# Hybrid decoder layer on one core: bias table read backwards by its user, per-tile roots of q and k, and several steps moved by a few slots

## Time and profile before

| what | value |
|---|---|
| median of 3 runs | 790.46 us (788.77 to 791.02) |
| profiled execution, own time | 790.41 us |
| its span | 788.7 us |
| mean granted TensorE clock | 0.969 |
| instructions in the span | 9486 |
| VectorE, ScalarE, GpSimd busy | 478.9, 338.8, 91.7 us |
| read of the bias table: issued, time to landing | 33.8 us, 8.0 us |
| first layer-norm transposes | 320.6 us |
| end of the plan (first feed-forward product) | 423.4 us |

### The profile page before, as it was taken

How to read it: one execution, slowest core, us unless ns; L and a number is a source line. 1 busy time by engine, 2 the same in 40 slices (tenths; PEclk the granted TensorE clock), 3 DMA queues, 4 the chain that set the end, 5 groups by cost and what they waited for, 6 DMA issues and landing times.

```text
span 788.7 us, 9486 instructions
## 1 busy us (share of the span) xinstructions
PE 738.3 (94%) x3442; PEld 588.2 (75%) x3446; DVE 478.9 (61%) x725; ACT 338.8 (43%) x508; POOL 91.7 (12%) x75
## 2 busy tenths in 40 slices
PE   3999978599989989799997999999999999999998
PEld 2766757477766778587875888888888888888886
DVE  5246797996799866666655565655656656222222
ACT  6244637187855576263334334344343443211110
POOL 2000364753100001303010000000000000000000
PEclk9999998799999999999996999999999999999999
DMA  8431132222211141102231133233332332333202
GB/s 260 151 139 55 54 106 54 54 62 91 63 53 54 55 160 54 53 16 92 81 108 53 54 106 84 78 105 106 106 96 74 96 106 106 107 106 107 82 26 106
DMA packets 78047, 69.46 MB, mean 88 GB/s; under 512 B 5815, under 2 KB 64535, under 8 KB 78015
## 3 DMA queue, kind: packets, MB, share of 16 engines
q1 hardware_dynamic: 77871, 68.51, 28.2%
q10 hardware_dynamic: 144, 0.52, 0.2%
HBM read 66.91 MB, written 2.12 MB: 88 GB/s over the span
## 4 chain that ended last, share of the span: by engine, by line
PE 72%; DVE 10%; issue 8%; ACT 4%; POOL 4%; DMA 1%; SPq 0%; DVEq 0%; POOLq 0%; ACTq 0%
PE bank L1454 62%; PE bank L1460 3%; POOL stats L730 3%; DVE u_acc L569 2%; PE bank L1474 2%; DVE w_lo L579 1%; DMA x_in<-in_x 1%; PE bank L1649 1%; PE bank L1625 1%; PE bank L1592 1%; DVE xbcT L1261 1%; DVE q_tok L1224 1%; POOL u_acc L751 1%; DVE k_tok L1224 1%; DVE h_lo L1090 1%
## 5 line engine op out<-in xcount | busy, mean ns | idle before, releaser
L1454 PE MATMUL bank<-h_hi,w_hi 128*128 128x512 f32 x480 | 191.3, 398 | 1.8 <-DVE h_lo L1090 1.8
L1454 PE MATMUL bank<-h_lo,w_hi 128*128 128x512 f32 x480 | 188.0, 392 | 0.0
L1454 PE MATMUL bank<-h_hi,w_lo 128*128 128x512 f32 x480 | 188.0, 392 | 0.0
L579 DVE TENSOR_TENSOR w_lo<-w_raw,w_hi 128x2048 fp32r<-128x2048 f32 x34 | 78.6, 2312 | 80.7 <-ACT w_hi L820 80.7
L1454 PEld LDWEIGHTS bank<-h_hi,w_hi 128*128 128x128 f32 x480 | 90.7, 189 | 28.4 <-issue 9.9
L1454 PEld LDWEIGHTS bank<-h_hi,w_lo 128*128 128x128 f32 x480 | 90.7, 189 | 19.6
L1454 PEld LDWEIGHTS bank<-h_lo,w_hi 128*128 128x128 f32 x480 | 90.9, 189 | 18.1
L1415 DVE SCALAR_TENSOR_TENSOR f<-bank,prm,f 128x511 f32<-128x511 f32 x88 | 65.8, 748 | 58.3 <-ACT f L1059 52.0
L820 ACT ACTIVATE w_hi<-w_raw 128x2048 fp32r<-128x2048 f32 x34 | 64.9, 1910 | 78.3 <-PE bank L1454 78.0
L1059 ACT ACTIVATE f<-bank,prm 128x512 f32<-128x512 f32 x44 | 33.8, 769 | 102.4 <-PE bank L1454 102.4
L1454 PE MATMUL bank<-w_hi,g_hi 128*128 128x512 f32 x176 | 68.5, 389 | 0.0
(11 more groups left out here) (231 smaller groups left out, 1049.8 us busy)
## 6 DMA issues: line engine op xcount, KB each, us to landing
w_raw<-in_w_up SPq DMA_DIRECT2D x44, 512.0 KB, 4.7
w_raw<-in_w_in SPq DMA_DIRECT2D x34, 512.0 KB, 4.6
w_raw<-in_w_down SPq DMA_DIRECT2D x22, 512.0 KB, 4.0
w_raw<-in_w_out SPq DMA_DIRECT2D x12, 512.0 KB, 4.3
x_in<-in_x SPq DMA_DIRECT2D x4, 512.0 KB, 6.8
trev<-distance_table SPq DMA_DIRECT2D x1, 2048.0 KB, 8.0
x<-in_x SPq DMA_DIRECT2D x4, 512.0 KB, 6.8
out_x<-y_out SPq DMA_DIRECT2D x8, 256.0 KB, 2.0
```

The source lines that it names most:

```text
L579: eng.tensor_tensor(wlo[:, slot, cols], wraw[:, slot, cols], whi[:, slot, cols].bitcast(F32), ALU.subtract).then_inc(ready, 1)
L1454: ins = pe.matmul(o, a, b, start=first and i == 0 and q == 0, stop=last and i == n - 1 and q == 2)
```

## The change

The one-hot table is made for distances the other way round, so that the read from memory lands directly in `tbias`, and `logit` reads a head's row backwards, from column W-1 to 0. `trev`, `jrev`, the `tbias` steps on TensorE and ScalarE and their two constants' instructions on GpSimd go. The read into `tbias`, which lies where x was, also waits for the four normalised tiles.

`qkms` and `qkn` are done per token tile: the tile's 8 sums are scaled in the slot that summed them, its root is 128 x 8, and its normalising stands ahead of the slot after the next.

Convolution taps of tiles 1, 2 and 3 end in slots 50, 63 and 65 instead of 52, 66 and 69. Layer norm moves from slots 70 and 71 to 66 and 67 (`lnn` follows one slot later), its transposes back from 73 and 74 to 70 and 71. The scan's four chunks start in slots 68, 72, 76 and 80 instead of 66, 70, 74 and 78. `silux` and `cs` move from slot 62 to 64, `xt` from 63 to 65, `siluz` from 68 to 70.

```diff
@@ -61,7 +61,7 @@
 
 def bucket_onehot():
 
-    n = np.maximum(511 - np.arange(NG), 0)
+    n = np.maximum(np.arange(NG) - (P - 1), 0)
     nf = np.maximum(n, 1).astype(np.float32)
     half = NBUCKET // 2
     large = half + (np.log(nf / np.float32(half)) / np.float32(np.log(MAXDIST / half))
@@ -72,9 +72,10 @@
 
 
 TOP_SLOTS = {1: (9, 36), 2: (9, 42), 3: (9, 48)}
-DW_SLOTS = [(15, 44), (14, 52), (42, 66), (46, 69)]
-LN_SLOT = 69
-SSD_SLOTS = (66, 70, 74, 78)
+DW_SLOTS = [(15, 44), (14, 50), (42, 63), (46, 65)]
+LN_SLOTS = (66, 66, 67, 67)
+LNT_SLOTS = (70, 70, 71, 71)
+SSD_SLOTS = (68, 72, 76, 80)
 DW_POOL = 0
 
 
@@ -143,15 +144,13 @@
         fill[TOP_SLOTS[b][1]].append(("sel", b))
 
     put(1, ("gtab",))
-    for h in range(NH):
-        put(11 + h, ("tbias", h))
 
     for w, what in enumerate("qk"):
         n = at[(what, 1)]
         for t in range(NT):
             put(n + 1 + t, ("qkev", what, t))
-        fill[n + 4].append(("qkms", what))
-        front[n + 7].append(("qkn", what))
+            fill[n + 1 + t].append(("qkms", what, t))
+            front[n + 3 + t].append(("qkn", what, t))
         put(n + 8, ("qkT", what, 0), ("qkT", what, 1))
         put(n + 9, ("qkT", what, 2), ("qkT", what, 3))
     for t in range(NT):
@@ -181,23 +180,22 @@
         spread([("dw", j, i) for i in range(CONV_K)], a, b)
         if j == DW_POOL:
             spread([("dwp", j, i) for i in range(1, CONV_K)], a - 1, b - 1)
-    d2 = LN_SLOT
     for t in range(NT):
-        put(d2 + 1 + t // 2, ("ln", t))
-        front[d2 + 2 + t // 2].append(("lnn", t))
+        put(LN_SLOTS[t], ("ln", t))
+        front[LN_SLOTS[t] + 1].append(("lnn", t))
     for j in range(4):
-        put(d2 + 4 + j // 2, ("lnT", j))
+        put(LNT_SLOTS[j], ("lnT", j))
 
     for m in range(8):
         n = at[("xbc", 0)] + 2 * m + 2
         put(n, ("xbase", m))
         put(n + 1, *[("xtap", m, i) for i in range(1, SK)])
-    s0 = at[("z", 0)] + 2
+    s0 = at[("z", 0)] + 4
     put(s0, ("silux",), ("cs",))
     put(s0 + 1, *[("xt", t) for t in range(NT)])
     for t in range(NT):
         put(at[("z", 1)] + 1 + t, ("ev", "z", t))
-    put(at[("z", 1)] + 4, ("siluz",))
+    put(at[("z", 1)] + 6, ("siluz",))
     for t, n in enumerate(SSD_SLOTS):
         put(n, ("csr", t))
         front[n + 1].append(("seg", t))
@@ -251,7 +249,7 @@
 
     for s in PLAN:
         k = s[0]
-        if k in ("prm", "tbias", "idx", "ln", "lnT", "qkT", "cs", "iwT", "yT"):
+        if k in ("prm", "idx", "ln", "lnT", "qkT", "cs", "iwT", "yT"):
             aux.append(s)
         elif k == "score":
             aux += [("score", s[1], e) for e in range(2)]
@@ -392,8 +390,6 @@
         oneh = at("onehot_sb", [NBUCKET, NG], F32, r5)
         relb = at("relb", [NBUCKET, NH], F32, r5 + 2560)
         gsb = at("gsb", [NH, NG], F32, r5 + 3 * K)
-        jrev = at("jrev", [P, P], F32, r5 + 6 * K)
-        trev = at("trev", [P, NH, 512], F32, r6)
         tbias = at("tbias", [P, NH, 512], F32, r2)
 
         iqT = at("iqT", [P, 2, SEQ], F32, r3)
@@ -667,7 +663,8 @@
 
                     finished(sp, "hT", NT - 1, 1)
                     src = bass.AP(gdram.tensor, 0, [[1, P], [NG, NH], [1, 512]])
-                    sp.dma_start(trev[:, :, :], src).then_inc(s_trev, 16)
+                    sp.wait_ge(xn_ready, NT)
+                    sp.dma_start(tbias[:, :, :], src).then_inc(s_trev, 16)
                 elif s == ("xt", 0):
 
                     for e in range(2):
@@ -716,14 +713,11 @@
             link(pool.affine_select(out=tri[:, :], in_=ones[:, :], compare_op=ALU.is_ge, fill=0.0,
                                     base=0, pattern=[[1, P]], channel_multiplier=-1))
             link(pool.memset(neg_l[:, :], 0.0))
-            link(pool.memset(jrev[:, :], 0.0))
             link(pool.affine_select(out=neg_q[:, :], in_=neg_l[:, :], compare_op=ALU.is_ge,
                                     fill=MASKED, base=0, pattern=[[-1, P]], channel_multiplier=1))
             link(pool.affine_select(out=neg_l[:, :], in_=neg_l[:, :], compare_op=ALU.is_ge,
                                     fill=MASKED, base=0, pattern=[[1, P]], channel_multiplier=-1))
-            pool.affine_select(out=jrev[:, :], in_=jrev[:, :], compare_op=ALU.not_equal, fill=1.0,
-                               base=-(P - 1), pattern=[[1, P]], channel_multiplier=1)\
-                .then_inc(s_const, 1)
+            pool.sem_inc(s_const, 1)
 
             def inverse_root(out_, in_, ready):
                 n = out_.free_size()
@@ -736,10 +730,9 @@
                     pool.wait_ge(ms_ready, t + 1)
                     inverse_root(rstd[:, t:t + 1], ssq[:, t:t + 1], rstd_ready)
                 elif k == "qkms":
-                    which = "qk".index(s[1])
-                    pool.wait_ge(qkms_ready, which + 1)
-                    inverse_root(rqk[:, 32 * which:32 * which + 32],
-                                 ssqk[:, 32 * which:32 * which + 32], rqk_ready)
+                    i = NT * "qk".index(s[1]) + s[2]
+                    pool.wait_ge(qkms_ready, i + 1)
+                    inverse_root(rqk[:, NH * i:NH * i + NH], ssqk[:, NH * i:NH * i + NH], rqk_ready)
                 elif k == "dw" and s[1] == DW_POOL:
 
                     _, j, i = s
@@ -882,9 +875,6 @@
                     act.activation(dtl, dtu, ACT.Ln).then_inc(dtl_ready, 1)
                 elif k == "hi":
                     split_hi(s[1])
-                elif k == "tbias":
-                    finished(act, *s)
-                    drain(act.activation(tbias[:, s[1], :], ps(*s)[:, :], ACT.Copy), *s)
                 elif k == "idx":
                     _, b, h = s
                     i = (b - 1) * NIH + h
@@ -1207,30 +1197,28 @@
                                       sqs[:, i % 2, :].rearrange("p (h c) -> p h c", h=NH),
                                       AX_X, ALU.add).then_inc(sq_used, 1)
                 elif k == "qkms":
-                    w = "qk".index(s[1])
-                    dve.wait_ge(sq_used, NT * (w + 1))
+                    i = NT * "qk".index(s[1]) + s[2]
+                    dve.wait_ge(sq_used, i + 1)
 
 
                     a, b = (1.0, HD * EPS) if s[1] == "q" else (1.0 / HD, EPS)
-                    c = ssqk[:, 32 * w:32 * w + 32]
+                    c = ssqk[:, NH * i:NH * i + NH]
                     dve.tensor_scalar(c, c, a, b, ALU.mult, ALU.add).then_inc(qkms_ready, 1)
                 elif k == "qkn":
-                    w = "qk".index(s[1])
-                    tok = q_tok if s[1] == "q" else k_tok
-                    dve.wait_ge(rqk_ready, w + 1)
-                    for t in range(NT):
-                        v3 = tok[:, t, :].rearrange("p (h c) -> p h c", h=NH)
-                        c = 32 * w + NH * t
-                        dve.tensor_tensor(v3, v3, rqk[:, c:c + NH].unsqueeze(2)
-                                          .to_broadcast([P, NH, HD]), ALU.mult).then_inc(qkn_ready, 1)
+                    _, what, t = s
+                    i = NT * "qk".index(what) + t
+                    tok = q_tok if what == "q" else k_tok
+                    dve.wait_ge(rqk_ready, i + 1)
+                    v3 = tok[:, t, :].rearrange("p (h c) -> p h c", h=NH)
+                    dve.tensor_tensor(v3, v3, rqk[:, NH * i:NH * i + NH].unsqueeze(2)
+                                      .to_broadcast([P, NH, HD]), ALU.mult).then_inc(qkn_ready, 1)
                 elif k == "logit":
                     _, u, b, hp = s
                     W = P * (b + 1)
                     if u == 0:
 
                         finished(dve, "qkT", "k", 3)
-                        for hh in range(NH):
-                            evacuated(dve, "tbias", hh)
+                        dve.wait_ge(s_trev, 16)
                     if u > 1:
 
                         finished(dve, "turn", u - 2, turn_banks((u - 2) // NPAIR) - 1)
@@ -1239,7 +1227,7 @@
                         finished(dve, "score", u, e)
                         drain(dve.tensor_tensor_reduce(
                             prob[:, u % 2, e, 0:W], ps("score", u, e)[:, 0:W],
-                            tbias[:, 2 * hp + e, 384 - P * b:384 - P * b + W], -1.0, 3.4e38, ALU.add, ALU.min, mn[:, i:i + 1]), "score", u, e)
+                            tbias[:, 2 * hp + e, W - 1::-1], -1.0, 3.4e38, ALU.add, ALU.min, mn[:, i:i + 1]), "score", u, e)
                 elif k == "share":
                     u = s[1]
                     dve.wait_ge(exp_ready, 2 * u + 2)
@@ -1586,11 +1574,6 @@
                                   first=whole or i == 0, last=whole or i == 1)
                     if whole or i == 1 or q == 3:
                         ins.then_inc(acc_step, 1)
-                elif k == "tbias":
-                    pe.wait_ge(s_trev, 16)
-                    claim(pe, *s)
-                    pe.matmul(ps(*s)[:, :], jrev[:, :], trev[:, s[1], :], start=True, stop=True)\
-                        .then_inc(aux_done, 1)
                 elif k == "idx":
```

## The result

The changed kernel takes 768.56 us (median of 4 executions, 767.84 to 770.06) against 789.62 for the kernel before (4 executions, 788.63 to 791.02): ratio 0.9734, 95% interval 0.9711 to 0.9758, that is 21 us less. The forecast was 763.6, range 755 to 775. The profiled execution is the slowest of the four, 770.06 us with a span of 768.3, so that the two traces differ by 20.4.

A forecast was written before the change was run, and what follows sets the result against it. TensorE's busy time and idle waits bound the kernel, with VectorE's queue setting the first stretch's pace once those waits go. 22.3 - 1.5 + 0 + 6.5 - 0.5 = 26.8 us off 790.4 gives 763.6, range 755 to 775.

The forecast's parts named there:

- Bias table: TensorE's eight pairs of products with the anti-identity go, 0.86 us each: 6.9 us.
- Reversed read: 32 logits on VectorE read the table with step -1: no change, bounds nothing and 15.6 us.
- Size of the roots: On GpSimd, a 128x8 root takes 2.25 us, bounds 0.6 and 8.
- Roots of q and k, the failed step: VectorE's queue up to the first logit: logit at 145.5 us, 20.3 earlier, with products at 0.94 us each.
- the first gain: Table and roots, up to the first softmax turn: gain 22.3 us, bounds 14 and 27.7.
- Conv taps: Six more VectorE taps in slots 44 to 62, on the softmax path: -1.5 us, between 0 and 4.5 lost.
- Silu: Silu, sums and xs transposes two slots later: new waits replace the probT wait, net 0, bounds -2 and +2.
- Layer norm: Ahead of the state-space steps: both u_tok waits and the slow quarter chunk go, gain 6.5 us, bounds 3 and 7.5.
- State-space steps: Two slots later, last ssm tile's transposes leave VectorE 3.7 us against TensorE's 3.1: -0.5 us, bounds 0 and -1.5.
- B: VectorE's backlog takes most of the first gain, products keep 1.65 us, taps cost 4.5: 774.9 us, chance 0.2.
- C: VectorE keeps up and TensorE reaches its ceiling: 37 us gained, 753 us, chance 0.1.
- E: GpSimd's eight roots hold VectorE as a port would, 18 us more on its queue: 781.6 us, chance 0.03.

The follow-up runs named there:

- late root: The changed kernel with GpSimd's root of each q and k tile one place later, behind that slot's conv tap: 764.41 us, ratio 0.9683.
- tile 0 late: The changed kernel with the conv taps of tile 0 in slots 32 to 62 instead of 15 to 44: 768.15 us, ratio 0.9741.
- without adds: The changed kernel with GpSimd's roots one place later and its 30 adds of conv tile 0 left out: 758.10 us, ratio 0.9619.

## Why the prediction was right or wrong

Right in sign, in size within 5 us (768.6 against 763.6), and in the order of the larger terms. Part of this closeness is luck: the first stretch fell 7.9 us short at the first turn, and the layer norm gave 2.5 more than its term.

- **Bias table**, 6.9 us: alone 7.7 (interval 6.3 to 8.9). Right. **Reversed read**, nothing: right, 687 ns against 689.
- **Size of the roots**, 2.25 us on the line between 128x1 and 128x32: the eight took 1.65 to 2.68 us, 2.11 in the mean. Right. The waits for q and k went as forecast, and the clock with them.
- **Roots of q and k, the failed step.** The prediction set VectorE's queue up to the first logit at 145.5 us: "some products still meet a tap: I take 0.94 us each and 0.7 us of small waits". The products took 0.92. The rest was wrong in two ways. First, the waits of VectorE were 5 us instead of 0.7, for it counted queues one by one and didn't ask what stands behind a GpSimd that waits; the late root gives 4.1 of the 5.4 us between forecast (22.3) and measurement (16.9) back. Second, it let only the normalising products meet GpSimd's adds. In the changed kernel the conv taps (17 in the stretch, 0.86 us in the mean against 0.73 where no add runs), the small scalings (0.29 against 0.16) and one w_lo split (3.25 against 2.28) met them too: 2.2 + 1.0 + 1.0 = 4 us. Also, "about 3.8 us are needed, so 2 more are recovered" didn't hold in the changed kernel: the first turn came 5.3 us behind the first logit. With table and roots alone, and with the late root, it was 3.8. With both causes away the first turn is at 147.0, 24.6 earlier than before, near the ceiling of 27.7 that the prediction named.
- **Conv taps**, -1.5: -2.1 in the attention stage, where VectorE's busy time rose from 96.9 to 102.2 us. The place is right; the denser taps as its cause are left by exclusion. Ahead of the first turn the term was too small: the prediction had one more tap there, 0.75 us. From the fourth w_lo split to the first turn it takes 83.6 us in the changed kernel and 80.3 with table and roots only; by the medians the moves cost some 1.3 us there. One more tap is what the traces show of it; the rest was not taken apart.
- **Silu**, 0: -0.9. The 2.44 us wait was foretold; that the quarter chunk behind it runs partly at the 1.2 GHz level (its products take 0.63 us each where 0.39 is usual) was not.
- **Layer norm**, +6.5: +9.0. Mis-sized: the waits of 5.4 and the slow quarter chunk behind them (1.6) went, and the counted loss of 0.5 for the fourth tile didn't come. A wait for yb of 0.8 us, which the prediction left out, went too. That makes 7.8; the last 1.2 us lie in shorter products here and there, and no run took them apart.
- **State-space steps**, -0.5: -0.4.
- **Rivals.** B (774.9: VectorE's backlog) had 14 for the first gain, and the first turn shows 14.4; but the products didn't keep 1.65 us, they took 0.92, and VectorE idled 5 us. C's ceiling for the first stretch was nearly reached, but only without GpSimd's adds. E, that roots hold up VectorE, is refuted: in the late-root trace the products beside roots take 0.68 us and the taps 0.73, as alone.

## What to carry to other kernels

When work is cut into pieces on a helper engine, don't ask only whether it keeps the pace; ask what stands behind each piece in its queue, and whether one of the pieces' inputs is made behind that. A queue that waits with ready work behind it, and an engine with 13% of the span that shows up in the chain, are the signs; one place further back was worth 4.1 us. Price VectorE's instructions by rows in which GpSimd does what it will do then, not by their mean over the span.

## What the runs showed of the hardware

- GpSimd's 128x8 to the power of -0.5 takes 2.1 us, 128x32 8.07, 128x1 0.56: a cost by column, small as it is.
- A GpSimd add of two SBUF tiles (1.1 us) and VectorE's instructions with two SBUF tiles as inputs take turns: taps 0.73 against 1.5 to 1.8, products 0.68 against 1.55. It goes both ways: the add at 130.41 us of the changed kernel, beside a tap, a product and a w_lo split, took 4.36. Four scalings of 128x8 beside adds took 0.47 to 0.87 with the late root, and 0.16 alone. The top-8 search and replacement aren't touched (0.68 at 512 columns either way).
- Beside a root VectorE isn't slowed (taps 0.74, products 0.68, a w_lo split 2.29), but the root is: 2.0 to 2.1 us in most places, and 4.21 where a product and a w_lo split of 2.29 ran beside it (97.66 us with tile 0 late, 99.29 without adds).
- The Trainium skill, SBUF — State Buffer, section Who interferes with whom, says that VectorE contends with a GpSimd instruction that reads SBUF where it has two SBUF inputs or uses a two-port mode, and not with one SBUF input outside these modes. The adds and the searches agree with it. The scalings have one SBUF input; whether they run in a two-port mode no row shows. Of the two-port modes the page says that who issues first has the shared ports for its whole instruction. If roots did so against taps, products and splits, these would wait for them, and by the rows above they don't.
- The logit instruction, fp32, reads its bias operand with step -1 as fast as with step +1, at 128 to 512 columns (687 against 689 ns at 512).
